# Strassen's method for the last 16 chunks of the up projection in a two-block transformer kernel on one core

## The reference

```python
def conv_ffn(xn, w_up, conv_w, conv_b, w_down):
    h = xn @ w_up
    a, b = jnp.split(h, 2, axis=-1)
    ...
    return (jax.nn.gelu(c, approximate=False) * b) @ w_down

h = h + conv_ffn(rmsnorm(h, ffn_norm_g[l]), ffn_w_up[l], ...)
```

## Time and profile before

| | |
|---|---|
| median of three runs | 1288.83 us |
| the profiled execution | 1291.47 us, its span 1289.7 us |
| PE (TensorE matmul) | 1253.3 us, 97% |
| PEld (weight load) | 1019.5 us, 79% |
| DVE (VectorE) | 699.2 us, 54% |
| ACT (ScalarE) | 568.5 us, 44% |
| POOL (GpSimd) | 530.7 us, 41% |
| HBM | 145 GB/s over the span |
| chain that ended last | PE 89%, DVE 4%, ACT 3%, POOL 2% |

### The profile page before, as it was taken

How to read it: one execution, slowest core, us unless ns; L and a number is a source line. 1 busy time by engine, 2 the same in 40 slices (tenths; PEclk the granted TensorE clock), 3 DMA queues, 4 the chain that set the end, 5 groups by cost and what they waited for, 6 DMA issues and landing times.

```text
span 1289.7 us, 20794 instructions
## 1 busy us (share of the span) xinstructions
PE 1253.3 (97%) x8570; PEld 1019.5 (79%) x8570; DVE 699.2 (54%) x1093; ACT 568.5 (44%) x870; POOL 530.7 (41%) x424
## 2 busy tenths in 40 slices
PE   6999999999999999999998899999999999999999
PEld 5788888866678888767786767788788888888999
DVE  3250004886431266686557657265565665766773
ACT  6541444786665233354544544353422221224452
POOL 6544454322234544534242126331444444546321
PEclk9999999999999999999999999999999999999999
DMA  9836795612115452412220013310222222224554
GB/s 387 348 131 243 248 230 191 163 50 97 51 66 188 122 163 79 181 66 76 69 107 16 3 66 131 135 61 34 99 98 98 81 87 94 99 88 172 166 185 151
DMA packets 24907, 165.05 MB, mean 128 GB/s; under 512 B 2792, under 2 KB 2920, under 8 KB 11504
## 3 DMA queue, kind: packets, MB, share of 16 engines
q1 hardware_dynamic: 20448, 128.15, 27.9%
q10 hardware_dynamic: 2064, 24.07, 5.0%
q0 software_dynamic: 2304, 11.54, 4.5%
HBM read 157.43 MB, written 29.38 MB: 145 GB/s over the span
## 4 chain that ended last, share of the span: by engine, by line
PE 89%; DVE 4%; ACT 3%; POOL 2%; issue 1%; DMA 0%; SPq 0%; DVEq 0%; ACTq 0%
PE banks L488 87%; PE banks L495 2%; DVE arena L1985 1%; POOL h_low L2557 1%; DVE arena L1982 1%; DVE arena L1987 1%; POOL weights_low L2557 1%; DMA arena<-in_mem 0%; ACT weights_high L1192 0%; ACT arena L1238 0%; ACT memory_high L1248 0%; ACT arena L1416 0%; ACT arena L1417 0%; ACT arena L1415 0%; DVE arena L1943 0%
## 5 line engine op out<-in xcount | busy, mean ns | idle before, releaser
L2499 POOL TENSOR_TENSOR weights_low<-weights,weights_high 128x512 fp32r<-128x512 f32 x324 | 433.2, 1367 | 580.5 <-ACT weights_high L1192 580.5
L488 PE MATMUL banks<-h_high_low,weights_high 128*128 128x512 f32 x880 | 358.2, 407 | 1.6 <-ACT arena L1443 1.6
L488 PE MATMUL banks<-h_low,weights_high 128*128 128x512 f32 x880 | 348.9, 397 | 0.0
L488 PE MATMUL banks<-h_high_low,weights_low 128*128 128x512 f32 x880 | 348.8, 396 | 0.0
L1192 ACT ACTIVATE weights_high<-weights 128x2048 fp32r<-128x2048 f32 (+2 forms) x90 | 156.3, 1737 | 243.1 <-PE banks L488 226.0
L488 PEld LDWEIGHTS banks<-h_high_low,weights_high 128*128 128x128 f32 x880 | 166.0, 189 | 46.0 <-issue 5.8
L488 PEld LDWEIGHTS banks<-h_low,weights_high 128*128 128x128 f32 x880 | 166.0, 189 | 41.8 <-issue 3.6
L488 PEld LDWEIGHTS banks<-h_high_low,weights_low 128*128 128x128 f32 x880 | 165.8, 188 | 40.4
L488 PE MATMUL banks<-arena 64*64 64x64 f32 (+6 forms) x1800 | 118.1, 263 | 4.1 <-issue 2.6
L488 PEld LDWEIGHTS banks<-arena 64*64 64x64 f32 (+3 forms) x1800 | 85.9, 148 | 29.9 <-issue 23.2
L1238 ACT ACTIVATE arena<-banks 128x256 f32<-128x256 f32 (+4 forms) x82 | 41.9, 519 | 53.4 <-PE banks L495 35.1
(11 more groups left out here) (360 smaller groups left out, 2371.9 us busy)
## 6 DMA issues: line engine op xcount, KB each, us to landing
weights<-in_stream SPq DMA_DIRECT2D x82, 1024.0 KB, 4.8
sums_kept<-in_down POOLq DMA_DIRECT2D x16, 704.0 KB, 12.8
arena<-in_ada SPq DMA_DIRECT2D x8, 1024.0 KB, 11.9
weights<-in_down SPq DMA_DIRECT2D x9, 704.0 KB, 4.1
weights<-sums_kept SPq DMA_DIRECT2D x9, 704.0 KB, 4.0
sums_kept<-in_down ACTq DMA_DIRECT2D x2, 2816.0 KB, 21.4
sums_kept<-sums_kept ACTq DMA_DIRECT2D x2, 2816.0 KB, 12.6
h<-sums_kept SPq DMA_DIRECT2D x7, 704.0 KB, 4.2
```

What stands on the lines that cost most here:

```text
L488: ins = nc.tensor.matmul(o, lhsT, rhs, start=start, stop=stop, skip_group_check=skip)
L2499: nc.gpsimd.tensor_tensor(lo_of(c)[:, cols], raw_of(c)[:, cols], hi_of(c)[:, cols].bitcast(F32), ALU.subtract).then_inc(sem("weights_split ...
```

## The change

The up projection's first three pairs (6 chunks) stay as they are. The other 16 chunks are left out of the stream (`STREAM` = 69), and their product is made by one level of Strassen's method. Inner dimension, output columns and tokens are halved; the output is cut into 16 units c of two 128-row tiles, where an even c is two tiles of a and an odd c the same two of b. Each unit is seven products of 4 blocks x 3 matmuls of 256 columns. What is added:

- The input is the normed one. VectorE makes `h_raw` anew from `xres`, `ffn_g` and `rms` (8 operations), then four sums of quarters (1024 elements a row), ScalarE seven high parts and VectorE seven low parts, all between the plain tiles. The plain part's input moves to other memory (`hf_raw`, `hf_lo`, `hf_hi`).
- The sums of up weights (`up_sums`, 4 x 4.19 MB in HBM) are made as the down weights' are: ScalarE issues four more copies of 4.19 MB (two behind line 1392's copy, one behind line 1496's, one before the RWKV part), GpSimd four more adds of 4 DMAs each; the waits on `sums_copied` and `sums_added` count these too.
- The 112 pieces (256 KB) come in 56 pairs, in six raw and four high places in the old slots. ScalarE makes all high parts, VectorE 5 of 7 low parts, GpSimd 2 of 7.
- Seven products lie in four banks; three are made on top of an earlier product, of which ScalarE first keeps a copy (`keep`). VectorE makes the four result quarters and one intermediate (`up_out`). The convolution's first tap goes from VectorE to ScalarE (`tap`), and the products with `rms` fall away for these tiles.
- In the down projection the order of sums and their places change: the sums of the second and fourth form are made by VectorE during the down projection instead of during the up projection, only every fourth piece is split by GpSimd (before: the first four as well), and the loads of the first five pieces wait for products 104, 108, 112, 112, 112 of the up projection.

The core of the diff:

```diff
+UP_PLAIN = 3
+UP = 2 * (KF // 2 - UP_PLAIN)
+STREAM = 63 + 2 * UP_PLAIN
+UP_STEPS = [[(c, f) for c, fs in ((i, (P1, R5)), (i - 1, (Q4, P3)), (i, (R7, P6, P2))) if 0 <= c < UP for f in fs]
+            for i in range(UP + 1)]
...
+        DOWN_FREE = [104, 108, UP_N, UP_N, UP_N]
+        DOWN_HI_FREE = [108, UP_N, UP_N, UP_N]
+        FROM_POOL = tuple(i for i in range(DOWN) if i % DOWN_PAIRS == 0)
```

TensorE:

```diff
+            for n, (c, f) in enumerate(UP_SEQ):
+                if f == P6:
+                    pe.wait_ge(sem("up_copied"), 2 * c + 1)
+                elif f == Q4:
+                    pe.wait_ge(sem("product_moved"), moved_at(c, SUM3))
+                elif f == P3:
+                    pe.wait_ge(sem("product_moved"), moved_at(c, C22))
...
+                for k in range(KH):
+                    last = k == KH - 1
+                    right = th_hi[f][:, k, :], th_lo[f][:, k, :]
+                    mm(o, whi[:, k, :], right[0], k == 0 and f not in (P6, Q4, P3), False, skip=True)
+                    mm(o, whi[:, k, :], right[1], False, False, skip=True)
+                    mm(o, wlo[:, k, :], right[0], False, last, sem("product_done") if last else None, skip=True)
```

ScalarE, before the stick-breaking steps; the code of the steps is as it was:

```diff
             act.wait_ge(sem("sums_added"), 2 * 16 * DOWN_PAIRS)
             act.dma_start(sums_kept[S2], sums_kept[S1]).then_inc(sem("sums_copied"), 16)
+            for to in (S1, S3):
+                act.dma_start(up_sums[to], up_in[A21]).then_inc(sem("sums_copied"), 16)
```

ScalarE, after them:

```diff
-            act.wait_ge(sem("sums_added"), 3 * 16 * DOWN_PAIRS)
+            act.wait_ge(sem("sums_added"), 5 * 16 * DOWN_PAIRS)
             act.dma_start(sums_kept[S4], sums_kept[S2]).then_inc(sem("sums_copied"), 16)
+            act.dma_start(up_sums[S2], up_sums[S1]).then_inc(sem("sums_copied"), 16)
```

ScalarE, before the RWKV part:

```diff
+            act.wait_ge(sem("sums_added"), 7 * 16 * DOWN_PAIRS)
+            act.dma_start(up_sums[S4], up_sums[S2]).then_inc(sem("sums_copied"), 16)
```

ScalarE, plain part of the up projection and its end:

```diff
+            split_weights()
+            for m in range(2):
+                gelu(m)
+            split_weights()
+            for i, f in enumerate(T_ORDER):
+                act.wait_ge(sem("token_made"), KD + 4)
+                high(th_hi[f], th_raw[f], sem("token_hi"))
+            split_weights()
...
+                        if f == (P1 if i < UP else Q4):
+                            gelu(up_tile(i - 2, 0))
+                        if f == (Q4 if i < UP else P3):
+                            gelu(up_tile(i - 2, 1))
...
+            for i in range(3):
+                down_high(i)
+            form_high(R5)
```

VectorE, plain part:

```diff
+            for m in range(2):
+                conv(m, True)
+            for k in range(KD):
+                stt(h_raw[:, k, :], xres[:, k, :], par("ffn_g", k), rms[:, :], ALU.mult, ALU.mult).then_inc(sem("token_made"), 1)
...
+            for m in range(2):
+                gact_plain(m)
+            for m in range(2, 4):
+                conv(m, True)
+            for i, f in enumerate(T_ORDER):
+                dve.wait_ge(sem("token_hi"), i + 1)
+                low(th_lo[f], th_raw[f], th_hi[f], sem("token_split"))
+            for m in range(2, 4):
+                gact_plain(m)
```

VectorE, results of a unit:

```diff
+                if f == P2:
+                    moved_(tt(to_tile(c, 0, 0), up_bank(c, P2), k1, ALU.add))
+                    dve.wait_ge(sem("up_copied"), 2 * c + 2)
+                    moved_(tt(k3, up_bank(c, R7), k2, ALU.subtract))
+                    dve.wait_ge(sem("product_moved"), moved_at(c, SUM3))
+                    moved_(tt(to_tile(c, 1, 1), k3, up_bank(c, R5), ALU.subtract))
+                elif f == Q4:
+                    moved_(tt(to_tile(c, 1, 0), up_bank(c, Q4), k2, ALU.subtract))
+                else:
+                    moved_(tt(to_tile(c, 0, 1), up_bank(c, P3), k2, ALU.add))
```

GpSimd:

```diff
-            add(S2, A11, 3)
-            low_weights(vb + 3, go)
-            add(S4, A12, 4)
-            low_weights(go, mixers + HI)
+            add(S2, A11, 5)
+            add(S1, A22, 5, True)
+            low_weights(vb + 3, vb + 4)
+            add(S3, A11, 5, True)
+            low_weights(vb + 4, go)
+            add(S4, A12, 7)
+            low_weights(go, go + 1)
+            add(S2, A11, 7, True)
+            low_weights(go + 1, mixers + HI)
```

More of the change, by code:

```diff
@@ L374, in build @@
+        th_lo = [hl11, ts_lo[0], hl22, ts_lo[1], hl12, ts_lo[2], hl21]
+        th_hi = [hh11, ts_hi[0], hh22, ts_hi[1], hh12, ts_hi[2], hh21]
+        kept1, kept2, kept3 = ([sums[:, i, TH * p:TH * (p + 1)] for p in range(2)] for i in range(3))
+        conv_in = at(SPARE + KH * TH * 6, 3, T + 2)
+        other = nF_rows
         whole = [ctx.enter_context(nc.psum_tensor(f"banks{b}", [P, 2 * T], F32))[:, :] for b in range(0, 8, 2)]
@@ L443, in down_loaded @@
             if s < RAW:
-                return loaded[s], 16 * ((STREAM + i % DOWN_RAW - 2) // RAW + 1 + turn)
+                return loaded[s], 16 * (sum(c % RAW == s for c in range(2, STREAM)) + turn + 1)
             return sem(f"first{s - RAW}_loaded"), 16 * (turn + 2)
@@ L1819, in _, with gelu, first_high_of @@
-            assert chunks[0] == STREAM + HI
-            for i in range(HI, DOWN):
+            def gelu(m):
+                act.wait_ge(sem("conv"), m + 1)
+                nc.scalar.activation(gact_raw[:, m, :], gact_raw[:, m, :], ACT.Gelu).then_inc(sem("gelu"), 1)
+            def first_high_of(m):
+                if m < DOWN_K:
+                    if m < 2 * UP_PLAIN:
+                        M.wait_out(act, ("up", m, 1))
+                    else:
+                        act.wait_ge(sem("forms_made"), made_at("gact", m))
+                    high(t_hi[0][:, m, :], q11[:, m, :], sem("forms_hi"))
@@ new lines, in _, with form_high @@
+            for _ in range(HI):
+                split_weights()
+            assert chunks[0] == STREAM + HI
+            def form_high(f):
+                act.wait_ge(sem("product_done"), UP_N + DOWN_PAIRS * (f - 1))
+                for g, (first, last) in enumerate(GROUPS):
+                    act.wait_ge(sem("forms_made"), {R5: made_at("T1", DOWN_K - 1), P6: made_at("T2", g), R7: made_at("T3", g),
+                                                    Q4: made_at("T4", g)}.get(f, made_at("gact", KF - 1)))
+                    high(t_hi[f % 2][:, first:last, :], form_raw[f][:, first:last, :], sem("forms_hi"))
@@ L1821, in _ @@
+            for i in range(3):
+                down_high(i)
+            form_high(R5)
+            for i in range(3, DOWN):
                 down_high(i)
@@ L1823, in _ @@
                 if p == 0 and 2 <= f < FORMS:
-                    act.wait_ge(sem("down_done"), DOWN_PAIRS * (f - 1))
-                    for g, (first, last) in enumerate(GROUPS):
-                        act.wait_ge(sem("forms_made"), 3 * DOWN_K + (g + 1 if f == 5 else 0))
-                        high(t_hi[f % 2][:, first:last, :], form_raw[f][:, first:last, :], sem("forms_hi"))
+                    form_high(f)
         @block.vector
@@ new lines, in conv @@
+            def conv(m, plain):
+                a, c = conv_in[:, m % 3, :], gact_raw[:, m, :]
+                if plain:
+                    if m >= 3:
+                        dve.wait_ge(sem("conv"), m - 2)
+                    o = M.full(dve, ("up", m, 0))
+                    tt(a[:, 2:T + 2], o, rms[:, :], ALU.mult).then_inc(M.out(("up", m, 0)), 1)
+                    M.wait_out(dve, ("up", m, 0))
+                    link(ts(c, a[:, 0:T], par("conv_w", m), par("conv_b", m), ALU.mult, ALU.add))
+                else:
+                    dve.wait_ge(sem("taps"), m - 2 * UP_PLAIN + 1)
+                link(stt(c, a[:, 1:T + 1], par("conv_w", KF + m), c, ALU.mult, ALU.add))
+                stt(c, a[:, 2:T + 2], par("conv_w", 2 * KF + m), c, ALU.mult, ALU.add).then_inc(sem("conv"), 1)
```

423 lines of the change are left out of this document (299 added, 124 removed).

## The result

| | before | after |
|---|---|---|
| median | 1288.92 us | 1296.20 us |
| lowest to highest | 1288.1 to 1290.3 | 1293.9 to 1298.8 |
| profiled execution, its span | 1291.47, 1289.7 | 1295.37, 1293.5 |
| TensorE busy | 97% | 96% |
| VectorE, ScalarE, GpSimd busy | 54%, 44%, 41% | 58%, 48%, 39% |

The ratio to before is 1.0056, with an interval of 1.0041 to 1.0070: slower, by 7.3 us of the medians.

What follows compares the result with a forecast made beforehand. TensorE was taken as the bound in the last stage. Terms -20.4 + 4.5 + 1.5 + 2.9 + 14.3 + 1.5 = +4.3 us against the profiled execution gave 1293 us on the median, range 1275 to 1306.

Steps and rivals of the forecast that it cites:

- Step 1: Strassen part of the up projection: 256-column matmuls spaced 0.118 to 0.120 us on TensorE, a gain of 20.4 us.
- Step 2: Seam ahead of the Strassen part: TensorE waits of 1 to 3 us at about 961, 975 and 987; 4.5 us taken.
- Step 3: Steady Strassen part: hardly any wait of TensorE for VectorE; 1.5 us taken.
- Step 4: Seam to the down projection: some 3 us of waiting, net loss of 2.9 us taken.
- Rival C: VectorE becomes the bound in the Strassen part through GpSimd's operations, +10 us: 1303 us; chance 0.10.
- Step 5: Near 241 us: TensorE gap of 14 us while ScalarE awaits a small store queued behind the copies; 14.3 us taken.
- The clock: After the stop near 241 us: part of the stretch at 1.2 GHz, costing 1.5 us.
- Rival B: Stick step 4: the store doesn't stop ScalarE, landing before 237.7 us; 1277 us, range 1271 to 1284; chance 0.18.

## Why the prediction was right

Predicted were 1293 us, and a loss behind the copies that is larger than the gain. Measured were 1296.2. By its steps:

- **Step 1, the slots: right.** The Strassen part runs from 1016.16 to 1176.45. Less the 0.85 us of waits in it, that is 159.4 us for 1344 matmuls, 0.1186 each; 0.1187 was taken from the earlier trace rows, and the gain of 20.4 us is there. The other sum, an estimate by the formula on the page "TensorE: Matmul & The Clock Gate" of the Trainium skill (section "Back-to-back issue gap"), has 146.7 us for this part (146.8 in the prediction, by rounding): the trace lies 12.7 us above it. The page gives that formula for an isolated matmul. The spacing of the trace of before carried over to matmuls that weren't in it.
- **Step 2, the seam ahead of the Strassen part: right place, term too large, 4.5 taken, 2.7 measured.** TensorE waited 0.45 us ahead of 979.96 and 2.23 ahead of 1004.86. Less the 18.6 us by which after is late there, these are two of the three places that were named (961 and 987; at 975 there was no wait). The mechanism was GpSimd beside VectorE, as said, and stronger than taken in the low parts; it was the waits that were fewer. VectorE's seven low parts, first and last of the seven, and GpSimd's two chunks beside them:

```profile
986.65 2.33 DVE L2045 TENSOR_TENSOR h_low<-h,h_high_low 128x1024 fp32r<-128x1024 f32 x1
...
1000.10 2.31 DVE L2045 TENSOR_TENSOR h_low<-h,h_high_low 128x1024 fp32r<-128x1024 f32 x1
```

```profile
986.12 17.41 POOL L2793 TENSOR_TENSOR weights_low<-weights,weights_high 128x512 fp32r<-128x512 f32 x8 [7.50 <-ACT weights_high L1304]
```

  The same width takes 1.22 us where GpSimd is idle. A split by itself takes some 1.25. Now the low parts start 2.24 us apart and the eight splits take 2.18 each, so each engine gets one operation done in the time in which the other does: they take turns, if not strictly, which would be 2.5. By the Trainium skill's page "SBUF — State Buffer" (section "Who interferes with whom") a VectorE instruction with two inputs in SBUF contends with a GpSimd instruction that reads SBUF, for ports that the two share under a lock. The trace agrees, and in the kernel with the piled splits too (0.68 became 1.21). The 6.70 us of the pile is more than one such turn: a split by itself is 1.3 us long.
- **Step 3, the steady part: right, with no wait but one at its end where 1.5 us were taken.** The one is 0.85 us, ahead of 1173.49, for a result of VectorE; it is counted in step 4. From 1025 to 1045 TensorE is busy 20.00 of 20 us and VectorE 16.54 (16.2 per two units of 19.9 were worked out). Rival C had a ground in the turns just shown, and still didn't come: in the Strassen part GpSimd works 6.35 us of 20 and the results read PSUM.
- **Step 4, the seam to the down projection: right.** 2.21 us at the start, 1.9 behind it and the 0.85 before it, 4.9 in all, against 2.4 of before: +2.5, with 2.9 taken. The reason given was only half right. The wait was put down to ScalarE's high part behind the GELU; when that was moved, VectorE was as late.
- **Step 5, the copies: right, and mis-sized by some 4 us.** The stop is 16.35 us and 0.74 behind it, 17.1, where 14.3 were taken. That it is the store that ScalarE waits for, and its packets behind the copies', came as said; that the weight chunk on SP's queue would land at 240.8 instead of 227.6 was not seen, and would have cost some 2 us even with the store in time. The store came in at 254.7 and not at 252: the rows gave 21, 29 and 39 us for the new bytes, 25 were taken, and 28 it was, near the rate of the earlier pair. The clock: 1.5 us were taken from the earlier trace rows, where the stop is one of 3 us; here the granted clock stayed at 0.50 until about 263.5, 5 us of work, and it cost 2.4. So the stage cost 19.5 us, where 15.8 were taken. The up projection starts 18.6 us later than in before: 0.8 that stood before the copies were issued, plus 19.5, less 1.7 that TensorE gains between 250 and 770 us. Little of that gain need be the change's: between 600 and 770 the kernel with half a copy, which has the same code there as before, gains 3.4 us on it, and the one with both copies loses 0.6.

The sum of the profiled executions is then -20.4 + 2.7 + 0 + 2.5, which is -15.2 where the starts show -14.8, and + 0.8 + 19.5 - 1.7: 3.8, as the spans differ. The forecast sum was 4.3. That it came so near is luck in part, errors that cancel: the seams and the steady part cost 3.7 us less than taken, the stop with its clock 3.7 more; the start's 0.8 and the later -1.7 were in no term. The 3 us between the forecast and the median are not in any step: against their medians the two profiled executions differ by 3.4 us. The stretch from 600 to 770, where alike kernels differ by up to 4 us, is where to look; more isn't shown.

Rival B (the store lands in time) is what the kernel with moved copies makes true: 1281, with a range of 1271 to 1284 given, and 1275.5 once GpSimd's pile is gone too. Its price was right; its condition wasn't met in the kernel as changed.

## What to carry to other kernels

A DMA that "runs beside" is free only until something small that somebody waits for stands behind it: list, for each big transfer, what is issued on the same queue after it, when its landing is awaited, and how many bytes are in flight on all queues by then, since the loads that others wait for slow down as well (1 MB of weights took 26 and 34 us here instead of 14). Move such a transfer behind the awaited one rather than onto another queue, and then look at what waits for the moved one, since that engine's whole program stands behind the wait. A reordering at a seam pays only where the moved operation is the last that is late; look at who is second before you try it.

## What the runs showed of the hardware

- A queue from ScalarE works off its DMAs in order, as far as these cases show: a store of 16 KB behind 11.3 MB landed 33.8 us after its issue, about when the second copy did, and its packets came behind those of the copies. Queues slow each other: with both new copies on GpSimd's, the 2.88 MB on ScalarE's took 28.3 us instead of 12.7, and 1 MB of weights on SP's 34.5 instead of 13.8 (26.2 with the copies on ScalarE's).
- After a stop of TensorE of 17 us the granted clock stayed at 0.50 for 5 to 7 us after work had begun again; with the waits behind it and the clock, the stop cost 19.5 us in the changed kernel and 21.2 in the old one.
- A 128x512 operation of VectorE in SBUF took 0.68 us beside twelve DMA issues of GpSimd, 1.21 beside a row of splits, and 6.70 beside both, where the splits too took 3.95 instead of 1.30. Why it takes both stays open.
